# Four more weight panels in seven block products, with their block sums made in DRAM

## Chip, cores and metric

The kernel runs on one core of a Trainium2 chip. The metric is the device time of one execution in microseconds. Engine names in the profile: PE is TensorE (PEld its weight loads), DVE VectorE, ACT ScalarE, POOL GpSimd, SP SyncE. DMAs are issued from queues of these engines; GpSimd's is the software queue (q0), SyncE's is q1.

## What is computed

One layer of a decoder trunk on 512 tokens with 1024 channels, all in f32, in three residual sub-layers and a final RMSNorm.

```python
h = rmsnorm(x, g_mix); za, zb, zc, zg = split(h @ w_in)
ya = chunked_spatial_gating(gelu(za), ...) @ w_branch_a
gb, gc, xin = split(zb);  yb = (gb * causal_conv3(gc * xin)) @ w_branch_b
yc = multiscale_pool(zc, c_wg, c_scale) @ w_branch_c    # windows 2, 4, 8, 16, minus token
gates = sigmoid(zg + b_gate)
x = x + (gates[0] * ya + gates[1] * yb + gates[2] * yc) @ w_o
x = x + cross_attention(rmsnorm(x), rmsnorm(mem))       # 4 heads, 256 memory tokens
x = x + (silu(gate) * up) @ w_ffn_out                   # gate, up = split(rmsnorm(x) @ w_ffn_in)
return rmsnorm(x, g_final)
```

## The kernel before

Weights come as panels of 128 x 2048 f32 (1 MB) into two slots of `raw`. Each f32 product is made of three matmuls (`mm3`): the high part of weights and activations, and each one's high part with the other's low part. So a panel is split twice on its way: ScalarE copies the high part (`split_hi`, rounding to fp32r), VectorE subtracts it (`split_lo`). `lo_ready` counts the panels whose low part is done; SyncE loads the next panel into a slot when the one before in it has been split. `panel_done` counts the panels that TensorE has finished.

The mixer's panels come in the order SV, SU (the spatial gating), GC, XI (the two convolution inputs), PC (pool), GB (the convolution's gate), and then for six steps `h` two gate panels and one branch panel (GA0 on). Panel numbers are constants: PC0 = 16, GB0 = 18, GA0 = 20. Up to GB each is done plainly by `fm_panel`: two tiles of 128 output channels, 8 blocks of the contraction, three matmuls of 512 columns, 48 in all.

The gate panels use Strassen's scheme in Winograd's form, with weights and tokens cut into 2 x 2 blocks: seven block products of 12 matmuls with 256 columns, 84 in all (`gate_seven`). This needs four sums of token blocks (`gth`, `gtl`, made once from X), four sums of weight blocks per panel, and kept parts of results. `gate_prep` on VectorE makes the low part of three plain blocks (`lo_a`) and then the four sums in `raw` itself; `gate_plain_hi` and `gate_pair_hi` on ScalarE make the high parts; `gate_prep_lo` the low parts of the sums (`lo_s13`, `lo_ready`). `keep` copies intermediate results from PSUM (s1, s5, u2, u3), which TensorE waits for before it adds on in the same place, and `gate_add` adds the kept parts on VectorE (`gate_sum`, `up_sum`). The high and low blocks in `blk` take the place of `wh` and `wl` and of X; there are two sets, so that a panel's plain high blocks wait for the end of the panel two before.

Each engine carries out its instructions in the order of the program, which is written out by hand. In the region of PC and GB, VectorE also makes the convolution's taps (`cv`), the trailing means (`pool_window`, g + 1 doubling steps and four short ones, lines 1191 to 1209), the product with the convolution's gate, and low parts (`pool_lo`, `actl`). ScalarE copies the pool's inputs to `zp`, and the high parts of all (`pool_hi`).

GpSimd starts 30 transfers at line 408 on, in 12 steps, which add blocks of the feed-forward's output weights in DRAM (`fo_sums`); the adding is done by the DMA (`accum_op`). They are wanted at the end of the kernel.

In the attention (lines 1891 to 1915) TensorE goes through the heads in a written-out order: scores, transposed probabilities, head outputs, and parts of the output panels (`out_part`) laid between. The transposes of head h wait for the low part `ol` of head h - 1, since they use its banks.

Of the kernel before, what the change touches and what calls it, by code (L numbers as in the profile page):

```python
# [28 lines left out]
P = 128  # L29
D = 1024  # L30
S = 512
# [12 lines left out]
NG = 12  # L44
# [40 lines left out]
def build(nc, first_in, weights, fo_in, x_in, xt_in, memt_in, cols_in, sgu_in, wg_in, ln_g_in, ln_b_in, gf_in, out):  # L85
    base = -(-nc.sbuf_base // 32) * 32

    kv_store = nc.dram_tensor("kv_store", (4, P, KT * M), F32).ap()
    fo_sums = nc.dram_tensor("fo_sums", (NP, P, 4, S), F32).ap()
# [25 lines left out]
    gsnap = at("gsnap", 200, [2, S])  # L115
    hole = lambda t: t[:, 0:4, S // 2:S].rearrange("p k (b f) -> p b k f", b=2)
# [85 lines left out]
    with ExitStack() as ctx:  # L202
# [29 lines left out]
        def landing(n):  # L232
            return 16 * (n // SLOTS - K0 // SLOTS + 1)
# [46 lines left out]
        fo_made = sem("fo_made")  # L280
# [46 lines left out]
        def _(sp):  # L327
# [12 lines left out]
            with sp.Fori(K0 // 2 + 1, FO0 // 2) as i:  # L340
                for s in range(SLOTS):
                    sp.wait_ge(lo_ready, 2 * i + (s - 1))
                    sp.dma_start(raw[:, s, :], weights[2 * i + (s - 2)]).then_inc(landed[s], 16)
            for q in range(2 * NP + 1):
# [6 lines left out]
                if q == 0:  # L351
                    sp.wait_ge(fo_made, 16 * 3 * NP)
# [18 lines left out]
        def _(pool):  # L371
# [22 lines left out]

            pool.wait_ge(panel_done, K0 + 1)
# [4 lines left out]
            for g in range(4):  # L400
                nc.gpsimd.affine_select(out=wsr[:, g, :], in_=wsr[:, g, :], compare_op=ALU.is_ge, fill=0.0, base=0,
                                        pattern=[[1, CHUNK]], channel_multiplier=-1).then_inc(ws_masked, 1)
            for t in range(TT):
                pool.wait_ge(var_ready, t + 3)
                rsqrt(small(RS + t), small(VR + t), 1).then_inc(rstd_ready, 1)

            pool.wait_ge(mixed, 4)
            pool.dma_start(wgr[:], wg_in).then_inc(wg_here, 16)

            made = 0  # L410
            for step in range(NP + 2):
                if step < NP:
                    pool.dma_start(fo_sums[step], fo_in[step, :, 0:4 * S].rearrange("p (b c) -> p b c", b=4)).then_inc(fo_made, 16)
                    made += 16
                if 1 <= step <= NP:
                    q = step - 1
                    pool.dma_start(fo_sums[q, :, 1:4, :], fo_in[q, :, 3 * S:6 * S].rearrange("p (b c) -> p b c", b=3),
                                   accum_op=ALU.add).then_inc(fo_made, 16)
                    made += 16
                if step >= 2:  # L420
                    q = step - 2
                    pool.dma_start(fo_sums[q, :, 0:4:2, :], fo_sums[q, :, 1:4:2, :], accum_op=ALU.add).then_inc(fo_made, 16)
                    made += 16
                pool.wait_ge(fo_made, made)
# [29 lines left out]
        def _(act):  # L454
# [130 lines left out]
            split_hi(XI0 + 2)  # L585

            for g in range(BT):
                act.wait_ge(a_fm, g + 1)
                copy(acth[:, g, :], bank[4 + g][:]).then_inc(acth_ready, 1)
            def gate_sigmoid(h, j, t):  # L590
                b, half = h // 2, h % 2
                i = 4 * half + 2 * j + t
                act.wait_ge(gate_sum if t == 0 else up_sum, 2 * h + j + 1)
# [1556 lines left out]
```

## Time and profile before

| | us |
|---|---|
| median of 3 runs (lowest, highest) | 886.72 (886.08, 887.08) |
| profiled execution | 886.68 |
| its span, first to last instruction | 884.7 |
| TensorE busy | 874.1 |
| VectorE busy | 649.1 |
| ScalarE busy | 419.8 |

The profile's page gives busy times by engine, shares by stretch, the chain of work that ended last, and groups of instructions. The trace behind it answers for single instructions (timeline), for who waited for whom, for busy times in a stretch, and for DMAs with the time from issue to landing. A matmul's duration overlaps that of the next one, so the pace of TensorE is read from starts. Matmuls stand under the lines of the helper `mm3` (1613 to 1615), high-part copies under line 455, low parts under line 980.

### The profile page before, as it was taken

What the parts mean: (1) busy time and instruction counts of PE and PEld (TensorE: products, weight loads), DVE (VectorE), ACT (ScalarE), POOL (GpSimd) and SP (SyncE); (2) the same over time, 40 slices, a digit from 0 to 9 for tenths busy, and PEclk for the clock granted to TensorE, in tenths of its full rate; (3) what the DMA queues carried; (4) which work ended last, traced back from release to release, by engine and by line L of the source; (5) the groups of instructions that cost most, each with busy time, mean ns of one, the idle gap of its engine ahead of it and who ended that gap; (6) DMA issues with size and microseconds to landing.
All of it is one profiled execution on the core that took longest, in us unless ns stands there. A gap on an engine that the chain in (4) does not pass through costs nothing.

```text
span 884.7 us, 13300 instructions
## 1 busy us (share of the span) xinstructions
PE 874.1 (99%) x5232; PEld 781.1 (88%) x5232; DVE 649.1 (73%) x825; ACT 419.8 (47%) x629; POOL 78.3 (9%) x89
## 2 busy tenths in 40 slices
PE   8999999999999999999999999999999999999997
PEld 7998888889999999988888788889999999988885
DVE  5684667689676687765455566898888888789877
ACT  6655432346444444533234332455554455467555
POOL 0101011211211000014200045000000000000000
PEclk9999999999999999999999999999999999999999
DMA  9946349889988423472221113213222232367522
GB/s 344 366 186 236 145 176 220 231 212 262 260 229 197 152 84 107 155 322 99 91 96 48 48 54 137 96 49 129 109 95 95 98 120 103 106 240 237 190 95 96
DMA packets 26012, 139.64 MB, mean 158 GB/s; under 512 B 2800, under 2 KB 2928, under 8 KB 13936
## 3 DMA queue, kind: packets, MB, share of 16 engines
q1 hardware_dynamic: 17728, 101.85, 31.8%
q0 software_dynamic: 6064, 25.17, 12.4%
q10 hardware_dynamic: 2176, 12.00, 3.5%
q8 instruction: 31, 0.51, 0.2%
q14 instruction: 13, 0.11, 0.0%
HBM read 132.72 MB, written 29.88 MB: 184 GB/s over the span
## 4 chain that ended last, share of the span: by engine, by line
PE 89%; DVE 6%; ACT 3%; issue 1%; DMA 1%; POOLq 0%; SPq 0%; POOL 0%; ACTq 0%; DVEq 0%
PE psum L1613 29%; PE psum L1615 29%; PE psum L1614 29%; DMA pack<-first 1%; DVE tl L980 1%; DVE wl L980 1%; ACT wh L455 0%; DVE fol L980 0%; PE psum L1865 0%; ACT pr L743 0%; PE psum L1665 0%; DVE w7l L980 0%; DVE sm L1325 0%; DVE hn L1400 0%; PE psum L1991 0%
## 5 line engine op out<-in xcount | busy, mean ns | idle before, releaser
L1613 PE MATMUL psum<-th,w7h 128*128 128x256 f32 x504 | 142.7, 283 | 0.3 <-ACT snap L455 0.3
L1614 PE MATMUL psum<-tl,w7h 128*128 128x256 f32 x504 | 142.6, 283 | 0.0
L1615 PE MATMUL psum<-th,w7l 128*128 128x256 f32 x504 | 142.6, 283 | 0.0
L980 DVE TENSOR_TENSOR wl<-raw,wh 128x2048 fp32r<-128x2048 f32 (+1 forms) x44 | 89.2, 2039 | 49.7 <-ACT wh L455 49.6
L1613 PEld LDWEIGHTS psum<-th,w7h 128*128 128x128 f32 x504 | 96.7, 192 | 0.5 <-issue 0.5
L1614 PEld LDWEIGHTS psum<-tl,w7h 128*128 128x128 f32 x504 | 96.8, 192 | 0.0
L1615 PEld LDWEIGHTS psum<-th,w7l 128*128 128x128 f32 x504 | 96.8, 192 | 0.0
L455 ACT ACTIVATE wh<-raw 128x2048 fp32r<-128x2048 f32 (+1 forms) x44 | 73.1, 1675 | 21.4 <-PE psum L1615 20.1
L1613 PE MATMUL psum<-hh,wh 128*128 128x512 f32 x192 | 75.0, 391 | 0.0
L1615 PE MATMUL psum<-hh,wl 128*128 128x512 f32 x192 | 74.8, 389 | 0.0
L1614 PE MATMUL psum<-hl,wh 128*128 128x512 f32 x192 | 74.7, 389 | 0.0
L455 ACT ACTIVATE snap<-psum 128x256 f32<-128x256 f32 x72 | 27.6, 383 | 84.2 <-PE psum L1615 80.9
L455 ACT ACTIVATE blk<-raw 128x1024 fp32r<-128x1024 f32 (+1 forms) x36 | 42.4, 1198 | 50.0 <-DVE raw L1171 25.4
L1613 PE MATMUL psum<-foh,hsh 128*128 128x512 f32 x156 | 61.6, 395 | 0.6 <-DVE fol L980 0.5
L1615 PE MATMUL psum<-foh,hsl 128*128 128x512 f32 x156 | 60.8, 390 | 0.0
L1614 PE MATMUL psum<-fol,hsh 128*128 128x512 f32 x156 | 60.8, 389 | 0.0
L1613 PE MATMUL psum<-gth,blk 128*128 128x256 f32 x192 | 54.4, 284 | 0.0
L1614 PE MATMUL psum<-gtl,blk 128*128 128x256 f32 x192 | 54.3, 283 | 0.0
L980 DVE TENSOR_TENSOR w7l<-psum,w7h 128x1024 fp32r<-128x1024 f32 x36 | 43.7, 1216 | 0.0
L1615 PEld LDWEIGHTS psum<-hh,wl 128*128 128x128 f32 x192 | 36.0, 188 | 7.6
L1614 PEld LDWEIGHTS psum<-hl,wh 128*128 128x128 f32 x192 | 36.1, 188 | 7.4
L1613 PEld LDWEIGHTS psum<-hh,wh 128*128 128x128 f32 x192 | 36.1, 188 | 7.3
(280 smaller groups left out, 2281.3 us busy)
## 6 DMA issues: line engine op xcount, KB each, us to landing
raw<-weights SPq DMA_DIRECT2D x68, 1024.0 KB, 4.8
fo_sums<-fo POOLq DMA_DIRECT2D x10, 1024.0 KB, 6.1
fo_sums<-fo POOLq DMA_DIRECT2D x10, 768.0 KB, 11.2
fo_sums<-fo_sums POOLq DMA_DIRECT2D x10, 512.0 KB, 14.9
raw<-fo_sums SPq DMA_DIRECT2D x10, 512.0 KB, 4.9
more<-fo_sums SPq DMA_DIRECT2D x10, 512.0 KB, 4.8
more<-fo SPq DMA_DIRECT2D x6, 512.0 KB, 3.7
pack<-first SPq DMA_DIRECT2D x3, 768.0 KB, 8.3
```

The lines of the kernel that those rows point to most:

```text
L455: copy = lambda o, i, **kw: nc.scalar.activation(o, i, ACT.Copy, **kw)
L980: return V.tensor_tensor(dst, v, f32(hi), ALU.subtract)
L1613: nc.tensor.matmul(dst, lh, rh, start=start, stop=False, **kw)
L1614: nc.tensor.matmul(dst, lh, rl, start=False, stop=False, **kw)
L1615: return nc.tensor.matmul(dst, ll, rh, start=False, stop=stop, **kw)
```

## The change

The pool's and the convolution gate's four panels are done in seven products too. Their weights are laid out as the gates' are. A new order of products, `seven_plain_first`, begins with three products that need plain blocks only; it is used for these four panels and for the first two gate panels, and `gate_seven` for the rest. For these six panels the sums of weight blocks are not made on VectorE: GpSimd makes them in DRAM (`w_sums`) in six steps of accumulating transfers, and SyncE loads them into the panel's slot once its plain blocks' low parts are made (`load_sums`). A panel of the six is thus loaded in two parts, 768 KB and 1 MB. Signs change: all sums of weight blocks are plain additions, the sums of token blocks carry the signs, and the right tile of each result comes out negated, which its reader undoes (`scale=-1.0`, `scalar=-1.0`).

The order on ScalarE and VectorE around these panels is written anew. The convolution gate's low parts (`conv_lo`) come later. The feed-forward's sums start once the last GB panel is done. In the attention the second output panel's first part comes before the transposes of head 2, head 1's part of the first panel behind head 2's output, and the split of the second output panel stands inside the softmax of head 2. Wait counts are renumbered. In the two long orders below (ScalarE's from `act.wait_ge(gtl_ready, 4)` on, VectorE's from `add_left(PC0, 0, 0)` on) the removed lines are left out.

```diff
-NG = 12
+NG = 16
+ND = 6
+NM = NG - ND
...
-            with sp.Fori(K0 // 2 + 1, FO0 // 2) as i:
+            def load_sums(n):
+                sp.wait_ge(lo_a, n - PC0 + 1)
+                sp.wait_ge(sums_made, made_for[n - PC0])
+                sp.dma_start(raw[:, n % SLOTS, :], w_sums[n - PC0].rearrange("p b f -> p (b f)")).then_inc(landed[n % SLOTS], 16)
+            for n in range(K0 + 2, GA0 + 4):
+                sp.wait_ge(lo_ready, n - 1)
+                cs = slice(4 * P, PANEL) if by_transfer(n) else slice(0, PANEL)
+                sp.dma_start(raw[:, n % SLOTS, cs], weights[n - 2, :, cs]).then_inc(landed[n % SLOTS], 16)
+                if by_transfer(n - 1):
+                    load_sums(n - 1)
+            with sp.Fori(GA0 // 2 + 2, FO0 // 2) as i:
                 for s in range(SLOTS):
                     sp.wait_ge(lo_ready, 2 * i + (s - 1))
...
+            def sums_step(step):
+                pool.wait_ge(sums_made, made[0])
+                if step < 3:
+                    a, n = 2 * step, PC0 + 2 * step - 2
+                    transfer(w_sums[a:a + 2], weights[n:n + 2].rearrange("n p (b f) -> n p b f", b=4))
+                if 1 <= step < 4:
+                    a, n = 2 * step - 2, PC0 + 2 * step - 4
+                    transfer(w_sums[a:a + 2, :, 0, :], weights[n:n + 2, :, 4 * P:8 * P], accum_op=ALU.add)
+                    transfer(w_sums[a:a + 2, :, 2, :], weights[n:n + 2, :, 0:4 * P], accum_op=ALU.add)
+                if 2 <= step < 5:
+                    a = 2 * step - 4
+                    transfer(w_sums[a:a + 2, :, 1, :], w_sums[a:a + 2, :, 2, :], accum_op=ALU.add)
+                if 3 <= step < 6:
+                    a = 2 * step - 6
+                    transfer(w_sums[a:a + 2, :, 3, :], w_sums[a:a + 2, :, 1, :], accum_op=ALU.add)
+            sums_step(0)
             pool.wait_ge(panel_done, K0 + 1)
...
             pool.dma_start(wgr[:], wg_in).then_inc(wg_here, 16)
-            made = 0
+            pool.wait_ge(panel_done, GA0)
...
+            act.wait_ge(gtl_ready, 4)
+            gate_plain_hi(PC0, 0)
+            pair_hi(PC0, 0)
+            gate_plain_hi(PC0 + 1, 1)
+            for g in range(BT):
+                act.wait_ge(a_fm, g + 1)
+                copy(acth[:, g, :], bank[4 + g][:]).then_inc(acth_ready, 1)
             keep(0, 0, "s1")
             keep(0, 0, "s5")
             keep(0, 0, "u2")
+            pair_hi(PC0 + 1, 1)
             keep(0, 0, "u3")
+            gate_plain_hi(GB0, 2)
+            padded(0)
             keep(1, 1, "s1")
+            pool_hi(0)
+            pool_hi(1)
             keep(1, 1, "s5")
             keep(1, 1, "u2")
+            pair_hi(GB0, 2)
+            keep(1, 1, "u3")
+            gate_plain_hi(GB0 + 1, 3)
+            padded(1)
+            keep(2, 0, "s1")
+            act.wait_ge(wg_here, 16)
+            copy(wgh[:], wgr[:]).then_inc(wgh_ready, 1)
+            keep(2, 0, "s5")
+            keep(2, 0, "u2")
+            pool_hi(2)
+            pair_hi(GB0 + 1, 3)
+            keep(2, 0, "u3")
+            gate_plain_hi(GA0, 4)
+            keep(3, 1, "s1")
+            keep(3, 1, "s5")
+            pool_hi(3)
+            keep(3, 1, "u2")
+            pair_hi(GA0, 4)
+            keep(3, 1, "u3")
+            gate_plain_hi(GA0 + 1, 5)
+            for i in range(4):
+                conv_hi(i)
+            keep(4, 0, "s1")
+            keep(4, 0, "s5")
+            keep(4, 0, "u2")
+            pair_hi(GA0 + 1, 5)
+            keep(4, 0, "u3")
+            keep(5, 1, "s1")
+            split_hi(GA0 + 2)
             for g in range(4):
                 act.wait_ge(c_scaled, g + 1)
                 copy(acth[:, 2 * BT + g, :], bank[4 + g][:]).then_inc(acth_ready, 1)
+            keep(5, 1, "s5")
+            keep(5, 1, "u2")
+            keep(5, 1, "u3")
...
+            def gate_prep(n, i):
+                w, blocks, p = raw_flat(n % SLOTS), raw_blocks(n % SLOTS), n % 2
+                dve.wait_ge(hi_a, i + 1)
+                lo(gate_lo[p][0], blocks[:, 1:4], gate_hi[p][0]).then_inc(lo_a, 1)
+                if by_transfer(n):
+                    return
+                dve.wait_ge(lo_a, i + 1)
+                chain(V.tensor_tensor(w[:, 2], w[:, 2], w[:, 0], ALU.add))
...
             for n in range(2):
-                split_lo(XI0 + n + 1)
                 if n == 0:
+                    split_lo(XI0 + 1)
                     token_sum_lo()
                 for t in range(2):
+                    if (n, t) == (0, 1):
+                        gate_prep(PC0, 0)
+                    elif (n, t) == (1, 1):
+                        gate_prep_lo(PC0, 0)
...
+            gate_prep(PC0 + 1, 1)
...
+            add_left(PC0, 0, 0)
+            gate_prep_lo(PC0 + 1, 1)
+            add_right(PC0, 0, 0)
+            gate_prep(GB0, 2)
             pool_window(0)
             pool_window(1)
             pool_lo(0)
             pool_lo(1)
+            add_left(PC0 + 1, 1, 1)
+            gate_prep_lo(GB0, 2)
+            add_right(PC0 + 1, 1, 1)
+            gate_prep(GB0 + 1, 3)
+            pool_window(2)
+            dve.wait_ge(wgh_ready, 1)
+            lo(wgl[:], wgr[:], wgh[:]).then_inc(wgl_ready, 1)
+            pool_lo(2)
+            add_left(GB0, 2, 0)
+            gate_prep_lo(GB0 + 1, 3)
+            add_right(GB0, 2, 0)
+            gate_prep(GA0, 4)
+            pool_window(3)
+            conv_gate(0)
+            conv_gate(1)
+            pool_lo(3)
+            gate_prep_lo(GA0, 4)
+            gate_add(GB0 + 1, 3, 1)
+            conv_gate(2)
+            conv_gate(3)
+            gate_prep(GA0 + 1, 5)
+            gate_prep_lo(GA0 + 1, 5)
+            gate_add(GA0, 4, 0)
...
+            for i in range(4):
+                conv_lo(i)
...
+            def seven_plain_first(n, i, j, free):
+                left, right = bank[2 * j], bank[2 * j + 1]
+                pe.wait_ge(lo_a, i + 1)
+                pe.wait_ge(*free)
+                gate_product(right[:, Q:S], n, 0, 1, "B11", start=True).then_inc(p1_done, 1)
+                gate_product(left[:, 0:Q], n, 0, 2, "B21", start=True)
+                pe.wait_ge(s1_kept, i + 1)
+                gate_product(right[:, 0:Q], n, 0, 0, "T4")
+                pe.wait_ge(lo_s13, i + 1)
+                gate_product(left[:, Q:S], n, 1, 0, "T1").then_inc(p5_done, 1)
+                gate_product(right[:, Q:S], n, 1, 1, "T2").then_inc(p6_done, 1)
+                pe.wait_ge(lo_ready, n + 1)
+                pe.wait_ge(s5_kept, i + 1)
+                gate_product(left[:, Q:S], n, 2, 1, "B22").then_inc(p3_done, 1)
+                pe.wait_ge(u2_kept, i + 1)
+                gate_product(right[:, Q:S], n, 2, 0, "T3").then_inc(panel_done, 1)
+            pe.wait_ge(gtl_ready, 4)
-                fm_panel(PC0 + n, h_hi, h_lo, first_tile, [(cx_ready, 2 * n + t + 1) for t in range(2)])
+                seven_plain_first(PC0 + n, n, n, (cx_ready, 2 * n + 2))
-                fm_panel(GB0 + n, h_hi, h_lo, first_tile, [(zp_ready, 2 * n + t + 1) for t in range(2)])
+                seven_plain_first(GB0 + n, 2 + n, n, (zp_ready, 2 * n + 2))
...
-                    gate_seven(GA0 + 3 * h + j, 2 * h + j, h, j)
+                    seven = gate_seven if h else seven_plain_first
+                    seven(GA0 + 3 * h + j, 4 + 2 * h + j, j, (low_read, 4 * h + 2 * j + 2))
...
             out_part(0, range(0, 2))
-            out_part(0, range(2, 4))
+            out_part(1, range(0, 2))
             transpose_probs(2)
             score(3)
             head_out(2)
-            out_part(1, range(0, 2))
+            out_part(0, range(2, 4))
+            out_part(1, range(2, 3))
             transpose_probs(3)
             out_part(0, range(4, 6))
             head_out(3)
-            out_part(1, range(2, 4))
+            out_part(1, range(3, 4))
             out_part(0, range(6, 8), True)
             out_part(1, range(4, 8), True)
```

## Rows read from the trace of the kernel before

**Rows 1.** The page: busy us, share of the span and instructions by engine.
```profile
PE 874.1 (99%) x5232; PEld 781.1 (88%) x5232; DVE 649.1 (73%) x825; ACT 419.8 (47%) x629; POOL 78.3 (9%) x89
```

**Rows 2.** Timeline of TensorE: start, duration (us), engine, line, operation, names, shapes.
```profile
146.58 0.47 PE L1613 MATMUL psum<-hh,wh 128*128 128x512 f32 x1
...
224.15 0.39 PE L1613 MATMUL psum<-acth,wh 128*128 128x512 f32 x1
...
224.83 0.28 PE L1613 MATMUL psum<-hh,blk 128*128 128x256 f32 x1
...
234.90 0.28 PE L1613 MATMUL psum<-hh,blk 128*128 128x256 f32 x1
```

**Rows 3.** TensorE around the pool's linear map; idle time in brackets.
```profile
192.04 0.39 PE L1615 MATMUL psum<-acth,wgl 128*128 128x512 f32 x1
...
192.60 0.50 PE L1613 MATMUL psum<-acth,wgh 128*128 128x512 f32 x1 [0.17 <-DVE actl L980]
```

**Rows 4.** Busy us of PE, PEld, DVE, ACT, POOL; granted clock, DMA share, GB/s.
```profile
147.00:214.00 67.00, 66.83 (x373) 58.28 (x372) 52.37 (x74) 29.61 (x40) 9.12 (x12) 1.00 0.89 228
```

**Rows 5.** Timeline of VectorE in the region that changes.
```profile
148.00 2.48 DVE L980 TENSOR_TENSOR actl<-psum,acth 128x512 fp32r<-128x512 f32 x4
...
162.43 0.70 DVE L1201 TENSOR_TENSOR wa<-zp 128x527 f32<-128x527 f32 x1
...
164.40 0.70 DVE L1201 TENSOR_TENSOR wa<-zp 128x527 f32<-128x527 f32 x1
...
182.31 1.76 DVE L980 TENSOR_TENSOR blk<-raw,blk 128x1536 fp32r<-128x1536 f32 x1 [0.68 <-ACT blk L455]
...
193.66 2.35 DVE L980 TENSOR_TENSOR blk<-raw,blk 128x1024 fp32r<-128x1024 f32 x2
...
204.61 0.69 DVE L1186 TENSOR_TENSOR psum<-psum,gsnap 128x512 f32<-128x512 f32 x1
...
211.48 2.28 DVE L980 TENSOR_TENSOR wl<-raw,wh 128x2048 fp32r<-128x2048 f32 x1
```

**Rows 6.** Timeline of ScalarE in the same region.
```profile
191.19 0.63 ACT L455 ACTIVATE acth<-zp 128x512 fp32r<-128x512 f32 x1 [2.90 <-DVE zp L1209]
...
194.32 1.47 ACT L455 ACTIVATE blk<-raw 128x1536 fp32r<-128x1536 f32 x1
...
195.70 0.36 ACT L455 ACTIVATE gsnap<-psum 128x256 f32<-128x256 f32 x1
...
201.25 2.00 ACT L455 ACTIVATE blk<-raw 128x1024 fp32r<-128x1024 f32 x2
```

**Rows 7.** Timeline of GpSimd: issues of the feed-forward sums' copies in DRAM.
```profile
124.20 0.54 POOL L413 DMA_DIRECT2D fo_sums<-fo  x1
...
158.37 0.54 POOL L413 DMA_DIRECT2D fo_sums<-fo  x1 [14.62 <-DMA fo_sums<-fo_sums]
```

**Rows 8.** Waits of GpSimd: engine, line, releaser, us in total, times, longest.
```profile
POOL acc L431 <- DVE X L1308: 102.6, 1, 102.6
```

**Rows 9.** Weight loads, median us to landing: all, then two short stretches.
```profile
raw<-weights SPq DMA_DIRECT2D x68, 1024.0 KB, 4.8
...
raw<-weights SPq DMA_DIRECT2D x1, 1024.0 KB, 6.8
...
raw<-weights SPq DMA_DIRECT2D x1, 1024.0 KB, 11.4
```

**Rows 10.** The chain that ended last, in the attention: start, us, piece.
```profile
488.12 0.47 PE psum L1613
...
501.21 1.06 PE psum L1865 x8
```

**Rows 11.** Timelines of ScalarE, VectorE and TensorE about the early weight panels.
```profile
38.81 2.01 ACT L455 ACTIVATE wh<-raw 128x1024 fp32r<-128x1024 f32 x2 [1.31 <-DMA raw<-weights]
...
52.08 2.35 DVE L980 TENSOR_TENSOR wl<-raw,wh 128x1024 fp32r<-128x1024 f32 x2
...
55.12 0.40 PE L1613 MATMUL psum<-wh,hh 128*128 128x512 f32 x1
```

More of the change, by code:

```diff
@@ L230, in of_piece, with by_transfer, landing @@
             return (panel, k // 4 + 1) if k % 4 == 3 else (piece, k + 1 - k // 4)
-        def landing(n):
-            return 16 * (n // SLOTS - K0 // SLOTS + 1)
+        def by_transfer(n):
+            return PC0 <= n < GA0 + 2
+        def landing(n, sums=False):
+            extra = min(max((n - PC0) // SLOTS, 0), ND // SLOTS)
+            return 16 * (n // SLOTS - K0 // SLOTS + 1 + extra + sums)
+        made_for = (192, 192, 224, 224, 240, 240)
         xt_here, memt_here = sem("xt_here"), sem("memt_here")
@@ L592, in gate_sigmoid @@
                 i = 4 * half + 2 * j + t
-                act.wait_ge(gate_sum if t == 0 else up_sum, 2 * h + j + 1)
+                act.wait_ge(gate_sum if t == 0 else up_sum, 4 + 2 * h + j + 1)
+                if h == 0:
+                    act.wait_ge(actl_ready, BT + 2 * j + t + 1)
                 if h in (1, 2):
@@ L613, in gate_pair_hi @@
             def gate_pair_hi(n, i, pair):
-                act.wait_ge(s2_ready if pair == 0 else s4_ready, i + 1)
+                if by_transfer(n):
+                    act.wait_ge(landed[n % SLOTS], landing(n, sums=True))
+                else:
+                    act.wait_ge(s2_ready if pair == 0 else s4_ready, i - ND + 1)
                 copy(gate_hi[n % 2][1 + pair], raw_blocks(n % SLOTS)[:, 2 * pair:2 * pair + 2]).then_inc(
@@ new lines, in gate_prep_lo, with add_left @@
+            def gate_prep_lo(n, i):
+                blocks, p = raw_blocks(n % SLOTS), n % 2
+                dve.wait_ge(hi_s13, i + 1)
+                lo(gate_lo[p][1], blocks[:, 0:2], gate_hi[p][1]).then_inc(lo_s13, 1)
+                if not by_transfer(n):
+                    dve.wait_ge(s4_ready, i - ND + 1)
+                dve.wait_ge(hi_ready, n + 1)
+                lo(gate_lo[p][2], blocks[:, 2:4], gate_hi[p][2]).then_inc(lo_ready, 1)
+            def add_left(n, i, j):
+                held = gsnap_first if i < 4 else gsnap
+                dve.wait_ge(p3_done, i + 1)
+                dve.wait_ge(u2_kept, i + 1)
+                V.tensor_tensor(bank[2 * j], bank[2 * j], held[:, 0, :], ALU.add).then_inc(gate_sum, 1)
@@ L1271, in _ @@
             for h in range(1, 6):
-                n, i = GA0 + 3 * h, 2 * h
+                n, i = GA0 + 3 * h, 4 + 2 * h
                 gate_add(n - 2, i - 1, 1)
@@ L1360, in _ @@
             pt_lo(1)
-            softmax(2)
+            softmax(2, between=lambda: split_lo(XO0 + 1))
             o_lo(1)
-            split_lo(XO0 + 1)
             pt_lo(2)
```

263 lines of the change are left out of this document (116 added, 147 removed).

## The prediction

> **What bounds the kernel now.** I read the page first: TensorE is busy for 874.1 of 884.7 us [rows 1], at the full granted clock (1.00) where I looked [rows 4], so time can only be won by issuing fewer columns or by closing the few gaps, and is lost at once if TensorE has to wait. A matmul's duration in the trace overlaps the next one, so I take the distance between starts. Three 512-column matmuls take 0.68 us and a seven-product panel of 84 matmuls with 256 columns takes 10.07 us [rows 2]: 0.2267 and 0.120 us each. One gap in the region that changes stands in the timeline: a matmul of the pool's linear map starts 0.56 us after the one before it instead of 0.23 [rows 3]. Then I read how full the other engines are there: from 147 to 214 us VectorE is busy for 52.4 of 67 us, ScalarE for 29.6 [rows 4]. VectorE has 14.6 us to spare, TensorE none.
>
> **The change, part by part.** I call the panels of the region A, B (pool, PC0 and PC0+1), C, D (convolution gate, GB0 and GB0+1), E, F (first gates, GA0 and GA0+1).
>
> TensorE's own work: a plain panel is 48 x 0.2267 = 10.88 us, a seven-product one 84 x 0.120 = 10.08. Four panels change: -3.2 us. The gap at 192.6 goes with its restart (0.33 + 0.11), and so do the slower starts at three other changes of operand, some 0.1 each, if nothing else is late: -0.8 together. The first branch panel ends at 224.83 [rows 2]; 48 matmuls and a restart earlier, at 213.8, it starts. With no new wait that would be 213.8 - 4.0 = 209.8 us.
>
> By the Trainium skill (TensorE: Matmul & The Clock Gate, Back-to-back issue gap) a matmul's start-to-start time is its columns at 2.4 GHz and about 2.5 ns. That would make the four panels save 4.8 us instead of 3.2. The rows show more than that for both shapes, and the sum goes by the rows.
>
> VectorE's work: four whole-panel `split_lo` of 2.21 go (-8.8) and the eight block sums of E and F at 0.7 (-5.6); in their place come four plain `lo` of 1.7 and four pairs of 2.3 (+16.0) and eight sums with the kept parts at 0.61 (+4.9) [rows 5]. Net +6.5: 58.9 us of work for a stretch that should shrink to 63. That is not over the limit, but now the order decides. ScalarE gets 1.5 + 2.0 instead of 1.9 for each of four panels and sixteen `keep` copies of 0.3 to 0.4 [rows 6]: +12 us, with room. But `keep` copies are waited for by TensorE inside a panel. In `seven_plain_first` s1 is needed 2.9 us after the panel's start, s5 7.2 us, and u2 8.6 us after it.
>
> So I lay the instructions out in their new order, with the durations of [rows 5, 6], 0.25 us from the end of a product to its reader, and 4.8 us for a panel's load while the software queue is quiet [rows 9]. A starts at 146.6 as before [rows 2], and ends at 156.7: its sums load at 137.6, well ahead.
> - B, s1: VectorE has done the convolution's taps and B's plain `lo` at 150.4 (the taps ended at 148.0 before [rows 5]; A's two `lo` now stand ahead of the last tile's). So B's sums land at 155.2. ScalarE copies them (157.2), then A's u3, C's plain blocks (1.4), two `zp` tiles (1.0) and s1: 160.3 against 159.5 needed. **+0.8.**
> - B, s5: it stands behind `pool_hi(1)`, which needs `pool_window(1)`. VectorE: B's pair of `lo` from 156.3 to 158.6, A's right sum 159.3, C's plain `lo` 160.9, window 0 (1.97 us [rows 5]) 162.9, window 1 (one level more, 2.70) 165.6, the pool copy 166.3, s5 166.7 against 164.6. **+2.1.** B ends at 169.6.
> - C, s1: behind B's u3, D's plain copy and two `zp` tiles after B's end: 173.0 against 172.5. **+0.5.** C ends at 180.2.
> - D, u2: behind `pool_hi(3)`, thus window 3 (4.17 us), which VectorE starts at 184.3 and ends at 188.6; u2 is kept at 189.6 against 188.8. **+0.8.** D ends at 191.1, the pool's linear map at 193.8, E at 203.9 without a wait.
> - F, s1: it waits for `gate_sum` of E, and `gate_add(GA0)` stands on VectorE behind F's `gate_prep_lo`, thus behind the load of F's sums. F's plain `lo` ends at 197.1 and releases that load. The software queue has just been given its first feed-forward copies, since D was done at 191.1. With a landing of 7.0 us (below) they are there at 204.1, copied at 206.0, lowered at 207.5, E's sum at 208.2, s1 at 208.7 against 206.7. **+2.0.** F ends at 215.9.
> - The branch panel needs `split_lo(GA0+2)`. From 207.5 VectorE has two sums (1.2), four scalings, four pool and four convolution `lo` (12 x 0.61 = 7.3) and this split (2.3) ahead [rows 5]: 218.4. **+2.5.**
>
> Sum of waits 8.7 against 4.0 won: the branch panel starts at 218.4 instead of 213.8, **+4.6 us**. In the stage behind it the gate panels keep their order and their work, so I let nothing be won back or lost there.
>
> The landing is the loosest term. Beside software-queue transfers the same 1 MB load took 6.8 us once and 11.4 us once, against 4.8 for the median of all [rows 9]; the 6.8 was issued between 126 and 127 us, some 2 us behind a copy like the new first one [rows 7], so I take 7.0. At 4.8 the region costs 2.4 instead of 4.6, at 11.4 it costs 9.0.
>
> The feed-forward sums start at about 191 instead of 124.2 [rows 7]. Before, GpSimd then waited 102.6 us for its next task [rows 8], which covers a delay of 67. I cost it at nothing; were the cover gone, the residual's sum of squares would be late by the excess.
>
> The six panels' sums, GpSimd's steps 0 to 5: A's and B's are asked for at 137.6. Of the feed-forward's steps of 2.3 MB one takes 14.6 us and its issues [rows 7]. By that pace steps 1 and 2 start near 50 and 66, step 3 behind the layer norm's powers at 88, and 4 and 5 are through by 130. The powers stand behind the wait of step 2, some 20 us before they are due: nothing. Step 0 is different. It copies 2 MB in DRAM right behind the powers for x and mem, and ScalarE waits for the load of a weight panel until 38.8 there; VectorE is then busy without a break until 54.4, and TensorE takes the result at 55.1 [rows 11]. So 0.7 us are free, and each further microsecond of that landing is lost. A load that was queued first seems to be served first (the 6.8 us one was behind the copy), so I take +0.3; bounds 0 and 2.5.
>
> Attention: two waits of TensorE for `ol` end at 488.1 and 501.2 [rows 10]. The first came because products of head 1 stood ahead of the second transposes; now head 0's products of the second output panel stand there, 2.72 us of them, whose weights are split during the exponentials. The last transposes wait for `ol` of head 2, until just before 501.2; with its scores 0.55 earlier that is 500.5, while TensorE has 1.36 us more work ahead of them and comes at 500.9. So the transposes come 0.3 earlier with 1.36 more done: **-1.6 us**. What is late next is nothing within 0.3 us. Bounds -1.9 and 0.
>
> Against the profiled run: 884.7 of span and 2.0 around it are 886.7, the same as the median of the runs. 886.7 + 4.6 + 0.3 - 1.6 = **890.0 us**.
>
> **Rivals.**
> 1. Faster: all of it is covered. ScalarE and VectorE spare 37 and 14.6 us in the stretch [rows 4], and if the kept copies come in time TensorE alone sets the pace: 886.7 - 4.0 - 1.6 = 881.1. It decides once window 1 ends 2.1 us earlier than laid out, before 163.5, and the other waits, which are shorter or come of the loads, fall with it. Against it: windows 0 and 1 stand in front of s5 whatever the transfers do.
> 2. The loads are not disturbed. F's sums land after 4.8 us: 887.8. For it: the median; against it: the queue is given its first copy six microseconds before that load.
> 3. They are disturbed as the worst row says, 11.4 us: 894.4.
> 4. The early copy is shared with the weight load. If the engines give each queue half, the rest of that load takes twice as long. An estimate for the rest is 2.5 us, as the copy is issued some five before 38.8 and needs two to begin: 38.8 becomes 41.3, less the 0.7 that is free 1.8 us, in place of 0.3: 891.5. Against it: the 6.8 us load came behind the copy, not beside it. The Trainium skill (DMA: Bandwidth & Descriptors, Queues, rings and completion order) says that each engine goes round its queues packet by packet; by that it would be this rival rather than the +0.3 of the sum, and no row here shows a copy that comes in behind a running load.
> 5. The sums in DRAM are not ready at 137.6, so that all is pushed back: each step would have to take 30 us. Hardly.
>
> **How the numbers follow.** Forecast 890.0: 0.45. Rival 1: 0.15; 2: 0.2; 3: 0.08; 4: 0.11; 5: 0.01. The range takes in 2 to 4, reaches 2.3 us below rival 2 for waits that come out shorter than laid out, and leaves most of 1 out: 885.5 to 894.5. A measurement tells 0.2%, 1.8 us, from no change. Faster: rival 1 and a little of 2, 0.18. Same: most of 2 and an edge of the forecast, 0.22. Slower: 0.60.
>
> **What would show it.** In the profile after: TensorE waiting for ScalarE's copies of the kept parts in B (twice), C, D and F, the longest near 166 us; a wait for VectorE's weights ahead of the branch panel near 218; the load of F's sums at 7 us or more; no wait at 488 and none at 501; TensorE busy for 3.2 us less. Wrong would be the forecast if the pool windows were done earlier than laid out, if s5 were not waited for at all, or if the first weight panels at 38 us came late by more than 1 us.

## The result and the profile after

The changed kernel takes 903.1 us (median of 4 runs, 901.53 to 904.29) where the kernel before takes 886.42 beside it: a ratio of 1.0186, 95% interval 1.0174 to 1.0198. By that ratio it is slower by 16.5 us, outside the predicted range. The profiled execution took 902.01 us with a span of 900.3 us, 15.6 us more than the 884.7 us of before.

Page of the changed kernel, busy us by engine, and TensorE's waits (line, releaser: us in total, times, longest):

```profile
PE 878.8 (98%) x5376; PEld 791.8 (88%) x5376; DVE 655.0 (73%) x833; ACT 430.6 (48%) x653; POOL 90.5 (10%) x104
```

```profile
PE psum L1739 <- DVE wl L1067: 4.8, 3, 3.4
PE psum L1739 <- DVE kl L1067: 3.2, 1, 3.2
PE psum L1739 <- ACT gsnap_first L504: 3.1, 4, 1.9
PE psum L1739 <- ACT gsnap L504: 2.0, 1, 2.0
```

Against [rows 1] TensorE is busy for 4.7 us more although it issues less work. The timeline of TensorE in the changed kernel says where it waited (idle time in brackets) and where the first seven-product panel and the first branch panel start:

```profile
46.72 0.39 PE L1739 MATMUL psum<-memh,wh 128*128 128x256 f32 x1 [3.40 <-DVE wl L1067]
...
71.80 0.80 PE L1739 MATMUL psum<-wh,hh 128*128 128x512 f32 x1 [3.25 <-DVE kl L1067]
...
156.60 0.36 PE L1739 MATMUL psum<-hh,blk 128*128 128x256 f32 x1
...
170.39 0.39 PE L1739 MATMUL psum<-gth,blk 128*128 128x256 f32 x1 [0.60 <-ACT gsnap_first L504]
...
176.85 0.35 PE L1739 MATMUL psum<-hh,blk 128*128 128x256 f32 x1 [1.88 <-ACT gsnap_first L504]
...
184.54 0.39 PE L1739 MATMUL psum<-gth,blk 128*128 128x256 f32 x1 [0.22 <-ACT gsnap_first L504]
...
201.09 0.39 PE L1739 MATMUL psum<-gth,blk 128*128 128x256 f32 x1 [0.45 <-ACT gsnap_first L504]
...
220.53 0.38 PE L1739 MATMUL psum<-gth,blk 128*128 128x256 f32 x1 [2.05 <-ACT gsnap L504]
...
230.27 0.50 PE L1739 MATMUL psum<-acth,wh 128*128 128x512 f32 x1 [0.80 <-DVE wl L1067]
```

PC0 starts at 156.6 instead of 146.58 [rows 2]: 10.0 us are lost before the first changed product. From there to the branch panel it is 73.7 us instead of 67.2: 6.5 more. The attention gives back some 1.5, and the rest of the 15.6 lies behind the last matmul. The two long waits at the top are new, and the engine runs at or near half clock behind them. Windows of the changed kernel (columns as in [rows 4]; the last three are granted clock, DMA share and GB/s):

```profile
46.70:51.00 4.30, 4.28 (x23) 4.28 (x24) 4.20 (x6) 1.94 (x4) 1.30 (x4) 0.60 0.63 204
71.80:74.80 3.00, 3.00 (x7) 2.42 (x8) 2.58 (x4) 1.53 (x3) 2.23 (x4) 0.50 1.67 614
156.60:230.30 73.70, 67.71 (x520) 66.03 (x518) 57.57 (x82) 36.58 (x62) 4.23 (x6) 0.95 0.64 205
177.30:180.50 3.20, 3.20 (x17) 3.20 (x16) 1.02 (x2) 1.56 (x2) 0.00 (x0) 0.50 0.00 0
221.60:225.00 3.40, 3.40 (x19) 3.40 (x18) 3.40 (x7) 2.63 (x5) 2.29 (x3) 0.50 0.98 361
```

A granted clock of 0.50 is 1.2 GHz instead of 2.4, so each microsecond of it costs half a microsecond: 1.6 and 1.7 us in the region, and 1.7 and 1.5 us behind the two early waits (VectorE's 57.6 us of work there had been put at 58.9).

The source of the early waits stands on ScalarE and GpSimd. Timeline of ScalarE, then of GpSimd, changed kernel:

```profile
44.35 2.00 ACT L504 ACTIVATE wh<-raw 128x1024 fp32r<-128x1024 f32 x2 [6.85 <-DMA raw<-weights]
...
66.32 2.01 ACT L504 ACTIVATE wh<-raw 128x1024 fp32r<-128x1024 f32 x2 [3.90 <-DMA raw<-weights]
```

```profile
33.11 0.70 POOL L423 DMA_DIRECT2D w_sums<-weights  x1
...
51.13 2.45 POOL L423 DMA_DIRECT2D w_sums<-weights  x3
```

The split that started at 38.81 before [rows 11] starts at 44.35, behind GpSimd's first copy; the one at 66.32 comes behind its second step, a copy and the first two accumulating transfers. And this is what the DMA queues moved between 39 and 42 us (packets, MB, share of the 16 engines):

```profile
q0 software_dynamic: 18, 1.05, 85.8%
q1 hardware_dynamic: 22, 0.18, 14.6%
```

Both queues finish about as many packets here, but the copy's are some 64 KB (1.05 MB in 18) and the weight load's 8 KB, so the copy gets six times the bytes. My theory after this: the 10 us are the two early steps in DRAM, and cost so much because of the copies' packet size; the 6.5 are an order that lets kept copies stand behind other things. Rivals: the copies cost by their 2 MB however cut; VectorE, with 57 us of work in 63, has no room for this change in any order.

### The profile page after: what moved, and what is told of

Its sections match the earlier page's. It is cut to its first block, busy times and chain, and to the rows that moved or that the text cites. A ratio compares the mean times of both kernels' runs of the same rounds, so it can differ in the third digit from the quotient of the medians.

```text
span 900.3 us, 13640 instructions
## 1 busy us (share of the span) xinstructions
PE 878.8 (98%) x5376; PEld 791.8 (88%) x5376; DVE 655.0 (73%) x833; ACT 430.6 (48%) x653; POOL 90.5 (10%) x104
## 4 chain that ended last, share of the span: by engine, by line
PE 76%; DVE 10%; DMA 7%; ACT 4%; issue 2%; SPq 0%; POOLq 0%; POOL 0%; ACTq 0%; DVEq 0%
PE psum L1739 25%; PE psum L1741 25%; PE psum L1740 25%; DMA raw<-weights 3%; DMA xt<-xt 2%; DMA raw<-w_sums 2%; DVE wl L1067 2%; DVE blk L1067 1%; ACT blk L504 1%; ACT wh L504 1%; DVE tl L1067 1%; DVE actl L1067 1%; ACT xt L548 0%; DVE fol L1067 0%; PE psum L2010 0%
## 5 line engine op out<-in xcount | busy, mean ns | idle before, releaser
L504 ACT ACTIVATE blk<-raw 128x1024 fp32r<-128x1024 f32 (+1 forms) x48 | 56.4, 1198 | 62.7 <-PE psum L1741 30.8
L1739 PE MATMUL psum<-gth,blk 128*128 128x256 f32 x256 | 73.8, 288 | 3.3 <-ACT gsnap L504 2.0
L1740 PE MATMUL psum<-gtl,blk 128*128 128x256 f32 x256 | 73.4, 287 | 0.0
L1739 PE MATMUL psum<-hh,blk 128*128 128x256 f32 x192 | 54.9, 286 | 1.9 <-ACT gsnap_first L504 1.9
L1067 DVE TENSOR_TENSOR blk<-raw,blk 128x1536 fp32r<-128x1536 f32 (+1 forms) x32 | 47.0, 1488 | 11.4 <-ACT blk L504 11.1
L1740 PE MATMUL psum<-hl,blk 128*128 128x256 f32 x192 | 54.7, 285 | 0.0
L1739 PEld LDWEIGHTS psum<-gth,blk 128*128 128x128 f32 x256 | 50.3, 197 | 4.1 <-ACT gsnap L504 2.2
L1740 PEld LDWEIGHTS psum<-gtl,blk 128*128 128x128 f32 x256 | 50.1, 196 | 0.0
L1739 PE MATMUL psum<-hh,wh 128*128 128x512 f32 x128 | 50.0, 391 | 0.0
L1741 PE MATMUL psum<-hh,wl 128*128 128x512 f32 x128 | 49.8, 389 | 0.0
```

The lines of the kernel that those rows point to most:

```text
L504: copy = lambda o, i, **kw: nc.scalar.activation(o, i, ACT.Copy, **kw)
L1067: return V.tensor_tensor(dst, v, f32(hi), ALU.subtract)
L1739: nc.tensor.matmul(dst, lh, rh, start=start, stop=False, **kw)
L1740: nc.tensor.matmul(dst, lh, rl, start=False, stop=False, **kw)
L1741: return nc.tensor.matmul(dst, ll, rh, start=False, stop=stop, **kw)
```

## The experiments

**1. The early copy alone, in the kernel before.**

```diff
+            pool.dma_start(w_copy, weights[PC0 - 2:PC0].rearrange("n p (b f) -> n p b f", b=4)).then_inc(copied, 16)
             pool.wait_ge(panel_done, K0 + 1)
```

> The kernel before, with one addition: GpSimd's first copy of 2 MB in DRAM (two weight panels into a tensor that nothing reads) behind the powers for x and mem, cut as in the changed kernel (16 pieces of 64 KB for each MB, where a weight load has 8 KB pieces). Theory T1, turns by packet: the software queue's large packets take some 85% of the engines while the copy runs, the weight load beside it lands in 12 to 13 us instead of 4.8, TensorE waits 3.5 us near 43 us and runs at half clock for a while behind it: +5.3, 892.0 us. Theory T2, the queues get half each: the load's rest takes twice as long, +1.8, 888.5 us. Theory T3, what was queued first is served first: +0.3, 886.9 us.

Measured: 892.46 us, ratio 1.0066 (1.0049 to 1.0082). ScalarE and TensorE, timelines of this run:

```profile
44.43 2.00 ACT L458 ACTIVATE wh<-raw 128x1024 fp32r<-128x1024 f32 x2 [6.88 <-DMA raw<-weights]
```

```profile
46.80 0.58 PE L1616 MATMUL psum<-memh,wh 128*128 128x256 f32 x1 [3.43 <-DVE wl L983]
```

One transfer that nobody waits for costs 6.2 us: 3.6 of waiting by distance between starts, and the rest behind it, where the clock was 0.50 for 6 us:

```profile
46.80:52.80 6.00, 6.00 (x28) 6.00 (x29) 5.90 (x9) 3.64 (x6) 1.79 (x4) 0.50 0.58 206
```

The time is within half a microsecond of T1's 892.0, and the cost three times that of equal shares. Of the 10.0 us that PC0 starts late in the changed kernel, this first copy alone accounts for 5.9 here.

**2. The same copy in 8 KB packets.**

```diff
-    w_copy = nc.dram_tensor("w_copy", (2, P, 4, 4 * P), F32).ap()
+    w_copy = nc.dram_tensor("w_copy", (2, P, 5, 4 * P), F32).ap()[:, :, 0:4]
```

> The kernel before with the same early copy of 2 MB as in the first experiment (892.46 us), but into rows of 10 KB of which 8 are used, so that it goes in 8 KB packets. Turns by packet: the weight load beside it gets about half of the engines, TensorE waits 0.5 to 1.2 us in all instead of 3.7, without a stretch at half clock: 887.4 us (886.8 to 888.2). If it is the 2 MB of traffic and not the packets that cost: 892.5 us.

Measured: 888.04 us, ratio 1.0014 (1.0004 to 1.0023). The load's reader on ScalarE, and the queues between 39 and 42 us:

```profile
40.35 2.01 ACT L458 ACTIVATE wh<-raw 128x1024 fp32r<-128x1024 f32 x2 [2.88 <-DMA raw<-weights]
```

```profile
q0 software_dynamic: 77, 0.63, 52.5%
q1 hardware_dynamic: 75, 0.61, 48.5%
```

The same 2 MB now cost 1.4 us by the medians, 888.04 against 886.6 (0.4 to 2.0 by the interval). Between 39 and 42 us the queues are nearly equal packet for packet in both runs (16 against 19 in run 1); with equal packets the bytes are too. Between 36 and 39 us they are not: the copy had 119 packets against 45 and 82% of the engines here as well, so turns by packet do not explain the first microseconds. The padding that makes the packets small also moves the rows' addresses apart; no run separates the two.

**3. Small packets in the changed kernel.**

```diff
-    w_sums = nc.dram_tensor("w_sums", (ND, P, 4, 4 * P), F32).ap()
+    w_sums = nc.dram_tensor("w_sums", (ND, P, 5, 4 * P), F32).ap()[:, :, 0:4]
```

> The changed kernel with one edit: the tensor of sums in DRAM gets rows of 10 KB of which 8 KB are used, so that the copies can't be joined into 64 KB packets and go in 8 KB packets like the weight loads. Bytes, order and waits are the same. T1 (turns by packet): the copies get about half of the engines instead of 85%; each early weight load lands in 8 to 10 us instead of 12 to 13, TensorE's two waits of 3.6 and 3.4 us near 43 and 68 shrink to 1 or less each and with them the stretches at half clock: 903.1 - 8 = 895 us (893 to 898). T2 (half each however the copy is cut): nothing changes, 903.1 us.

Measured: 894.89 us, 1.0092 (1.0076 to 1.0109): 8.2 us less than the changed kernel. PC0 starts at 147.51, 9.1 us earlier, and the stretch from there to the branch panel takes 77.7 us, 4.0 longer. A new wait appears (TensorE, this run):

```profile
152.64 0.39 PE L1739 MATMUL psum<-gth,blk 128*128 128x256 f32 x1 [2.01 <-ACT gsnap_first L504]
```

A's s1 stands on ScalarE behind the block copies of A's sums, whose load lands in 8.3 us beside GpSimd's last steps. The early loss had hidden that. B's wait for s1 also grew from 0.60 to 1.92 and F's from 2.05 to 3.61, while B's for s5 shrank from 1.88 to 0.40.

The second early wait has gone too, but not because its load met smaller packets. In the changed kernel that panel's load was issued at 54.7 us, behind GpSimd's second step (51.1 to 53.6), since the first wait had made it late. Here the first wait is short, the load goes out at 50.5, ahead of the step, and ScalarE splits the same panel at 58.22. The next load, behind the step, is slow with 8 KB packets too; its reader has the room. The load in the changed kernel, then the two of this run and the split:

```profile
raw<-weights SPq DMA_DIRECT2D x1, 1024.0 KB, 11.6
```

```profile
raw<-weights SPq DMA_DIRECT2D x1, 1024.0 KB, 4.8
raw<-weights SPq DMA_DIRECT2D x1, 1024.0 KB, 10.6
58.22 2.00 ACT L504 ACTIVATE wh<-raw 128x1024 fp32r<-128x1024 f32 x2
```

**4. No sums made at all.**

```diff
-                sp.wait_ge(sums_made, made_for[n - PC0])
-                sp.dma_start(raw[:, n % SLOTS, :], w_sums[n - PC0].rearrange("p b f -> p (b f)")) ...
+                sp.dma_start(raw[:, n % SLOTS, :], weights[n - 2]) ...
...
-            sums_step(0)
...
-            sums_step(5)
```

> The changed kernel without GpSimd's making of the weight sums: the six panels' second load reads a weight panel instead, 1 MB as before, so the sums are not those of the reference. All early software-queue traffic is gone but the small loads. If the early 10 us are the copies' and nothing else's, PC0 starts at 146.6 us again and the time is 903.1 - 10.0 = 893.1 us; the waits in B, C, D and F (6.0 us and some 3.2 of half clock) stay. If something else in the change delays the start, more than 895 us.

Measured: 890.84 us, 1.0054 (1.0037 to 1.0072). TensorE's start of PC0:

```profile
146.15 0.36 PE L1733 MATMUL psum<-hh,blk 128*128 128x256 f32 x1
```

All of the early 10 us come of GpSimd's transfers. The run is 2.3 us faster than expected; the wait for s5 in B is 1.88 us here too, but the windows behind it show the full clock, which is 1.6 of them.

**5. Kept copies ahead of the pool's high parts.**

```diff
-            pool_hi(0)
-            pool_hi(1)
             keep(1, 1, "s5")
             keep(1, 1, "u2")
+            pool_hi(0)
+            pool_hi(1)
...
-            pool_hi(3)
             keep(3, 1, "u2")
+            pool_hi(3)
```

> The changed kernel with ScalarE's order changed in two places: the kept copies s5 and u2 of the second pool panel stand ahead of the high parts of pool windows 0 and 1, and u2 of the second convolution-gate panel ahead of that of window 3. If the copies wait only because they stand behind the windows, TensorE's wait of 2.04 us in B and its half clock behind it (1.6) and the 0.61 in D go: 903.1 - 4.2 = 898.9 us. If VectorE is the bound there (57.6 us busy in the 73.7 of this stretch), it is late elsewhere instead and most of it comes back: 902 us or more.

Measured: 900.14 us (899.23 to 907.15), ratio 1.018 (1.0138 to 1.0223). That is 3.0 less than the changed kernel by the medians, but the intervals overlap, and in the profile 1.35 of it lies ahead of PC0 (155.25 instead of 156.60), where the edit changes nothing. The stretch itself takes 72.4 us instead of 73.7. B's wait for s5 and D's for u2 are gone, and part of it comes back (TensorE, C and F):

```profile
180.29 0.39 PE L1739 MATMUL psum<-gth,blk 128*128 128x256 f32 x1 [0.94 <-ACT gsnap_first L504]
...
217.77 0.58 PE L1739 MATMUL psum<-gth,blk 128*128 128x256 f32 x1 [3.76 <-ACT gsnap L504]
```

**6. Feed-forward sums after F.**

```diff
-            pool.wait_ge(panel_done, GA0)
+            pool.wait_ge(panel_done, GA0 + 2)
```

> The changed kernel with one number changed: GpSimd starts the feed-forward sums once the second gate panel F is done, not once the second convolution-gate panel D is. If the load of F's sums (7.5 us) is slow for the first of these copies, it lands in 4.8 to 5 us, TensorE's wait of 2.2 us for s1 in F goes with its half clock (1.6), while the wait ahead of the branch panel grows from 1.0 to some 2 us, since VectorE's work ahead of it only moves by 2.7: 903.1 - 2.7 = 900.4 us (899.4 to 901.4). If the late landing is not the copies' doing, or the sums now come too late for the end of the kernel, 903 us or more.

Measured: 901.39 us (900.32 to 903.54), ratio 1.0177 (1.0161 to 1.0192). The landing of F's sums in the changed kernel and in this one:

```profile
raw<-w_sums SPq DMA_DIRECT2D x1, 1024.0 KB, 7.5
```

```profile
raw<-w_sums SPq DMA_DIRECT2D x1, 1024.0 KB, 4.8
```

and what TensorE then waited for in this one:

```profile
226.75 0.50 PE L1739 MATMUL psum<-acth,wh 128*128 128x512 f32 x1 [1.94 <-DVE wl L1067]
```

F's wait is gone, the branch panel's grew from 0.80 to 1.94, and the half clock moved with it (0.63 over the 3.45 us behind the wait). The stretch takes 71.1 us instead of 73.7, and the clock behind the branch panel's wait takes most of that back. By the medians 1.7 us are won, but this is not clear of the noise (the intervals overlap), and PC0 started 1.0 earlier for no reason of the edit. The mechanism is shown, its gain is not. No new wait appears at the end of the kernel.

**7. The attention alone, in the kernel before.** The edit is the change's own, in the last lines of its diff.

> The kernel before with the change's attention order alone (the order of the parts of the two output panels, and the second panel's split inside the softmax of head 2). My term of the sum: -1.6 us, 884.8 us (884.5 to 885.3), no wait of TensorE for the low part of a head's output any more. Rival: VectorE's split in the softmax delays the probabilities and the gain is gone, 886.4 us or more.

Measured: 885.43 us, ratio 0.9987 (0.9978 to 0.9996), 1.2 us less; the forecast 1.6 lies within the interval. Neither wait of [rows 10] is there.

**8. The edits of 3, 5 and 6 together.**

> The changed kernel with the three edits together: 8 KB packets for the sums, kept copies ahead of the pool's high parts, feed-forward sums after F. From 894.9 us with small packets alone: in B 2.1 us of wait and 1.7 of half clock go, in D 0.9, in F 3.8 and 1.7; the wait for A's sums (2.2, their load took 8.3 us beside GpSimd's last steps) stays, some 0.7 comes back in C and 1.5 ahead of the branch panel: 894.9 - 10.2 + 2.2 = 886.9 us (885.5 to 889). If VectorE is the bound of the stretch, it stays above 890 us.

Measured: 891.96 us, 1.0058 (1.0042 to 1.0073), above the whole range that I had summed and by the limit written beforehand the rival's figure. TensorE waits in A, B, C and ahead of the branch panel:

```profile
151.96 0.39 PE L1739 MATMUL psum<-gth,blk 128*128 128x256 f32 x1 [1.14 <-ACT gsnap_first L504]
...
164.15 0.49 PE L1739 MATMUL psum<-gth,blk 128*128 128x256 f32 x1 [1.85 <-ACT gsnap_first L504]
...
176.92 0.38 PE L1739 MATMUL psum<-gth,blk 128*128 128x256 f32 x1 [0.95 <-ACT gsnap_first L504]
...
220.45 0.50 PE L1739 MATMUL psum<-acth,wh 128*128 128x512 f32 x1 [2.29 <-DVE wl L1067]
```

**9 and 10. An order for each kept copy.** Against 8 (main lines; lines that a move takes away are left out):

```diff
+                if n == GB0 + 1:
+                    load_sums(n - 1)
...
             gate_plain_hi(PC0 + 1, 1)
+            keep(0, 0, "s1")
...
             keep(0, 0, "u3")
+            keep(1, 1, "s1")
...
             split_lo(GA0 + 2)
+            for i in range(4):
+                conv_lo(i)
```

and in 10 against 9:

```diff
-            sums_step(0)
...
             pool.dma_start(wsr[:], sgu_in).then_inc(ws_here, 16)
+            sums_step(0)
```

> The changed kernel with 8 KB packets, feed-forward sums after F, and ScalarE's and VectorE's orders in the region written so that each kept copy stands where its product ends (s1 of A, B, C and E ahead of block copies, B's plain low part ahead of the last taps, the low half of the first branch panel ahead of the convolution's low parts; the sums of C are loaded before D's plain blocks). TensorE's waits there (1.3, 2.0, 1.1, 0.5 and 2.4 us in the kernel with the three edits, 891.96 us) should shrink to 1.5 together: 892.0 - 5.8 = 886.2 us (884.5 to 888). If VectorE, which has some 58 us of work in 63, is the true bound of the stretch, the waits move but stay: 890 us or more.

> The same with GpSimd's first copy issued some 5 us later, behind the three small loads at 37 to 39 us, when the weight load that ScalarE waits for at 38.8 has mostly landed. Of the 1.1 us that TensorE still waits near 49 and 55 us half or more should go, while the sums of A are asked for at 138 and should still be made in time: 0.6 us less than the run before, 885.6 us. If the next weight load is hit instead, or A's sums now come too late, it is no faster.

Measured: 891.63 and 891.01 us, no better than 8; the later first copy left 1.07 us of the 1.15 of early waits. One long wait had taken the place of those in A, B and C, by my own order. TensorE and ScalarE of run 9:

```profile
185.04 0.58 PE L1743 MATMUL psum<-gth,blk 128*128 128x256 f32 x1 [4.19 <-ACT gsnap_first L506]
...
219.67 0.47 PE L1743 MATMUL psum<-acth,wh 128*128 128x512 f32 x1 [2.01 <-DVE actl L1071]
```

```profile
181.07 2.00 ACT L506 ACTIVATE blk<-raw 128x1024 fp32r<-128x1024 f32 x2 [1.66 <-DMA raw<-w_sums]
```

D's s1 stood behind a block copy that waited for a load; and the branch panel asked for eight low parts where it reads four.

**11. Those two mended.** Against 9 (main lines):

```diff
+            keep(2, 0, "u3")
+            keep(3, 1, "s1")
             pool_hi(2)
             pair_hi(GB0 + 1, 3)
-            keep(2, 0, "u3")
...
-            keep(3, 1, "s1")
...
             pool_window(2)
+            add_left(GB0, 2, 0)
+            add_right(GB0, 2, 0)
...
-                        pe.wait_ge(actl_ready, 2 * BT)
+                        pe.wait_ge(actl_ready, 2 * BT if b else BT)
```

> The first reordered kernel (891.63 us) had two waits of TensorE left in the region: 4.35 us for s1 of D, whose copy stood on ScalarE behind the block copies of D's sums, and 2.17 us ahead of the branch panel, which asked for all eight low parts though its own four were long made. Here C's sums are added behind window 2, u3 of C and s1 of D stand ahead of D's block copies, and the branch panel waits for the four it reads. Both waits and the half clock behind them (1.6 us each) should go: 891.6 - 4.3 - 2.2 - 3.0 = 882.1 us (881.5 to 885), faster than both kernels, as the sum for covered waits said (881.1 and 1.1 for the early copy). If there is no room on VectorE, a new wait of over 1 us appears at the start of E or F and it stays above 885 us.

Measured: 889.3 us, 1.0035 (1.0021 to 1.0049). Smaller waits in D, the pool's linear map, E and F:

```profile
183.99 0.38 PE L1742 MATMUL psum<-gth,blk 128*128 128x256 f32 x1 [1.93 <-DVE hh L1070]
...
192.82 0.50 PE L1742 MATMUL psum<-acth,wgh 128*128 128x512 f32 x1 [0.75 <-DVE actl L1070]
...
198.04 0.39 PE L1742 MATMUL psum<-gth,blk 128*128 128x256 f32 x1 [1.40 <-ACT gsnap L506]
...
210.08 0.39 PE L1742 MATMUL psum<-gth,blk 128*128 128x256 f32 x1 [1.70 <-ACT gsnap L506]
```

D's is a load that GpSimd has no part in: the sums were issued at 173.45 right behind E's plain blocks in the same queue.

```profile
raw<-w_sums SPq DMA_DIRECT2D x1, 1024.0 KB, 8.2
```

**12. Loads in the order of need, the pool's linear map behind E.** Against 11 (main lines):

```diff
-                if n == GB0 + 1:
+                if GB0 < n < GA0 + 3:
                     load_sums(n - 1)
                 sp.wait_ge(lo_ready, n - 1)
...
             pool_window(3)
-            conv_gate(0)
-            conv_gate(1)
-            pool_lo(3)
-            gate_prep_lo(GA0, 4)
             gate_add(GB0 + 1, 3, 1)
+            gate_prep_lo(GA0, 4)
...
+                    if h == j == 0:
+                        pool_linear()
```

> The second reordered kernel (889.3 us) waits 2.08 us in D for its sums, whose load took 8.2 us behind the 768 KB of E's plain blocks in the same queue, 0.91 for the last pool window, and 1.56 and 1.86 in E and F for s1, whose sum stands on VectorE behind the next panel's block sums. Here the pool's linear map stands behind E instead of before it, each panel's sums are loaded ahead of the next panel's plain blocks, the gate's product with the first two tiles stands behind C's sums, and the sums of D and E ahead of the low parts that wait for loads. If these waits come of order alone, at most 1.5 us of the 6.4 stay: 889.3 - 4.9 = 884.4 us (883 to 886), faster than before. If VectorE's 57 us of work in this stretch are its bound, they move again and it stays at 887 us or more.

Measured: 883.85 us (882.57 to 884.31, 5 runs), ratio 0.9964 (0.995 to 0.9978): 2.5 us faster than the kernel before and 19 faster than the changed one. TensorE starts PC0 and the branch panel, with one wait of over 0.3 us between them; the last line is the window of the stretch:

```profile
148.02 0.36 PE L1741 MATMUL psum<-hh,blk 128*128 128x256 f32 x1
...
161.54 0.39 PE L1741 MATMUL psum<-gth,blk 128*128 128x256 f32 x1 [0.32 <-ACT gsnap_first L506]
...
212.53 0.40 PE L1741 MATMUL psum<-acth,wh 128*128 128x512 f32 x1
```

```profile
147.40:211.00 63.60, 63.25 (x512) 62.11 (x511) 57.97 (x80) 39.07 (x62) 0.00 (x0) 1.00 0.45 166
```

The stretch takes 64.5 us instead of 67.2. VectorE has 58 us of work in it and TensorE hardly waits, so the rival of a VectorE without room is wrong, though runs 8, 9 and 11 had all come out above the limits written for it: it was the order, and in one place a wait for more low parts than were read. The edits of 9 to 12 were not run one by one, so what each is worth is not shown. What is left of GpSimd's early transfers (PC0 at 148.0, not 146.6) is 1.4 us. So the 2.5 us won are 2.7 of the stretch and 1.2 of the attention (experiment 7), less 1.4.

## Why the prediction was wrong

- **The early copy**: the step that failed. The sum gave +0.3 with bounds 0 and 2.5 for GpSimd's step 0, and nothing for step 1 beside a load; together it was 10.0. The forecast's own sign of being wrong came true: the split of 38.81 came 5.5 us late. Three things in it were wrong. I took the queue that was there first as served first, from a single load of 6.8 us [rows 9]; run 2 shows the queues sharing the engines about equally between 39 and 42 us, with the load there first. Rival 4 had turns, but as half the bytes each, which is near what equal packets give (run 2 costs 1.4 us, rival 4 said 1.8); with 64 KB against 8 KB it is about six to one in the changed kernel and five to one in run 1 (6.2 us). The diff showed the difference: the new copy is contiguous on both sides, while `fo_sums` has a strided source (30 packets for 0.25 MB between 129 and 132 us of the kernel before), and I compared them as if alike. And I priced one load: the first wait made a later load go out behind the second step, where it took 11.6 us, and the clock fell behind both waits. That wait comes of the first; the packet size did little there (10.6 us with small ones). The Trainium skill says (DMA: Bandwidth & Descriptors, Queues, rings and completion order) that engines go round the queues by packet. The 77 against 75 and 18 against 22 packets between 39 and 42 us agree with it, if its packets are those of the profile, which is not shown; the 119 against 45 between 36 and 39 us of run 2 do not. I had cited it and turned it into shares of bytes.
- **The bounds** of that term were the larger failure: the profile of before had no contiguous copy beside a load, and I let the guess of half shares be nearly the upper end. It did have eleven weight loads beside the feed-forward's copies, between 126 and 245 us: nine took 6.7 to 11.5 us and two 4.9. I read two of them, and the 7.0 for F's load, near the best of the nine, came out at 7.5 by luck as much as by reading. The rows had no ground for a cap below "the load waits until the whole copy is done", about the copy's own duration.
- **The waits in the region**: right in place and nearly in size. Predicted B 0.8 and 2.1, C 0.5, D 0.8, F 2.0, branch 2.5, 8.7 together; by distances between starts they were 0.75, 2.04, 0.38, 0.61, 2.21 and 0.96, 6.95 together. The branch's was smaller; F, delayed by the half clock, needs it later, which would explain it, but no run shows that alone.
- **The half clock** was missing: 3.3 us in the region and 3.2 early. I counted waits as their own length, and so had +4.6 us for the region, which took 6.5.
- **TensorE's own work**, -4.0: 6.5 = 6.95 + 3.3 - 3.8, and run 12 almost without waits gives -2.7 with some 0.5 of waits left, -3.2. Right within 0.8 us. By the issue gap of the Trainium skill (TensorE: Matmul & The Clock Gate, Back-to-back issue gap) it would have been 1.6 more, and the rows were the better guide.
- **Attention**, -1.6: -1.2 with 0.4 to 2.0 in the interval. **The later feed-forward sums**, nothing: no new wait at the end, in the changed kernel or in run 6, where they start 20 us later still.
- **Rival 1** (all covered, 881.1) was not the changed kernel, but run 12 comes within 2.8 us of it, 1.4 of which is the copy.

The sign of TensorE busy for 3.2 us less did not come either: it was 4.7 more, with the half clock in it.

What stays open: whether the packets' size alone or also the rows' new addresses made the first copy cheap, why the copy takes 82% of the engines in its first 3 us even in 8 KB packets, and why the clock fell behind some waits and not behind others as long.

## What to carry to other kernels

A transfer that nobody waits for is not free while weights are streamed: ask what its packets are, not only its bytes, and break a contiguous copy into pieces no larger than those of the load it meets. That helped the load that was under way; one issued behind the small pieces and the accumulating transfers still took twice its time (10.6 us), so see also which load a delay pushes behind the next transfer. In a chain of three engines a copy that TensorE waits for must not stand behind one that waits for a load or for VectorE, and taking one such wait away shows the next: price the order to the end of the stretch before you change one line. When no row shows a collision, its upper bound is the whole of the other transfer.

## What was new about the hardware

- Two queues on the same engines, between 39 and 42 us, finished about as many packets each: 18 packets of 64 KB against 22 of 8 KB (85.8% and 14.6% of the engines), and 77 against 75 with 8 KB on both sides (52.5% and 48.5%). Three microseconds earlier it was 119 against 45 with 8 KB on both sides.
- Padding a tensor in DRAM, so that rows of 8 KB no longer adjoin, made the packets small at the same bytes. It took a single copy's cost from 6.2 to 1.4 us (experiments 1 and 2) and the changed kernel's time down by 8.2 us (experiment 3).
- Behind a wait of 1.88 us in B the granted clock was 0.50 for 3.2 us in the changed kernel; behind the same 1.88 us in experiment 4 it was 1.00. Waits of 1.93, 1.40 and 1.70 us in experiment 11 had the full clock behind them.
